# A hybrid decoder step on one core: lists ranked side by side, six raw buffers late in the value pass, and one convolution piece moved

## The reference

```python
xn = rmsnorm(x);  q, k, v, val, gate = split(xn @ w_in)
A  = sliding_window_attention(q, k, v)          # window 128, 8 heads, 2 key heads, learned sinks
glu = val * sigmoid(gate)                       # 512 channels
C  = silu(layer_norm(causal_depthwise_conv31(glu))) @ pw
h  = x + concat(rmsnorm(A), rmsnorm(C)) @ w_out
y  = h + PEER(rmsnorm(h))
```

```python
s = einsum(q, keys)                              # token, head, half, 128 keys
ts, ti = top_k(s, 16)                            # 16 lists of 128 for each token
best, pos = top_k(ts[half 0] + ts[half 1], 16)
act = gelu(u[idx] @ x) * softmax(best);  y = act @ v[idx]
```

## Time and profile before

| | |
|---|---|
| median of 3 runs | 1666.12 us (1665.33 to 1666.69) |
| profiled execution | 1666.06 us |
| its span | 1664.2 us |
| PE busy | 1622.5 us, 97% of the span |
| DVE busy | 1406.8 us, 85% |
| ACT busy | 825.9 us, 50% |
| DMA over the span | 480.42 MB, 289 GB/s mean |

### The profile page before, as it was taken

The page is one execution under the profiler, slowest core; times in us unless marked ns, Lnnn a source line. Parts: engine busy times, 40 slices in busy tenths (PEclk is TensorE's granted clock), DMA queues, the critical chain, the costliest instruction groups (busy, mean ns, idle before and its releaser), DMA issues.

```text
span 1664.2 us, 23162 instructions
## 1 busy us (share of the span) xinstructions
PE 1622.5 (97%) x8269; PEld 1387.7 (83%) x8269; DVE 1406.8 (85%) x2709; ACT 825.9 (50%) x1361; POOL 564.5 (34%) x414
## 2 busy tenths in 40 slices
PE   8998999999999999999999999999999999999998
PEld 6875555687999999999999999997777777777787
DVE  2178877877878999989999999969988989889896
ACT  5532333342244444449999999963333333333332
POOL 0000000010003344435454554534545545545450
PEclk9999999999999999999999999999999999999999
DMA  7113322253437899988999999999999999999994
GB/s 221 56 51 39 30 76 89 65 170 121 150 112 292 327 318 343 359 286 329 396 392 399 395 402 394 404 400 401 397 395 403 404 403 397 403 403 392 404 374 155
DMA packets 154504, 480.42 MB, mean 289 GB/s; under 512 B 25951, under 2 KB 42783, under 8 KB 152215
## 3 DMA queue, kind: packets, MB, share of 16 engines
q1 hardware_dynamic: 96791, 252.43, 42.9%
q0 software_dynamic: 55296, 201.35, 31.6%
q10 hardware_dynamic: 2304, 25.17, 3.6%
HBM read 424.99 MB, written 53.64 MB: 288 GB/s over the span
## 4 chain that ended last, share of the span: by engine, by line
PE 73%; DVE 13%; DMA 9%; ACT 2%; issue 2%; POOL 0%; DVEq 0%; SPq 0%; ACTq 0%; POOLq 0%
PE ps L858 26%; PE ps L1002 20%; DMA raw<-in_v 8%; PE ps L978 5%; PE ps L812 5%; PE ps L617 5%; PE ps L601 5%; DVE lo L1617 3%; PE ps L688 2%; DVE acc L1783 1%; DVE ring L1779 1%; ACT hi L1126 1%; DVE cacc L1463 1%; PE ps L629 1%; PE ps L640 1%
## 5 line engine op out<-in xcount | busy, mean ns | idle before, releaser
L1126 ACT ACTIVATE hi<-raw 128x1024 fp32r<-128x1024 f32 x236 | 249.6, 1058 | 367.5 <-PE ps L1002 232.1
L1387 POOL DMA_INDIRECT ring<-in_u,idx x192 | 271.8, 1415 | 421.8 <-DVE hu L1779 263.3
L1387 POOL DMA_INDIRECT ring<-in_v,idx x192 | 280.1, 1459 | 266.9 <-DVE acc L1783 253.7
L1617 DVE TENSOR_TENSOR lo<-raw,hi 128x1024 fp32r<-128x1024 f32 x236 | 288.6, 1223 | 87.3 <-ACT hi L1126 74.1
L858 PE MATMUL ps<-xh,lo 128*128 128x384 f32 x1024 | 342.7, 335 | 0.0
L858 PE MATMUL ps<-xh,hi 128*128 128x384 f32 x864 | 295.1, 342 | 4.2 <-DVE lo L1617 4.2
L858 PE MATMUL ps<-xl,hi 128*128 128x384 f32 x864 | 288.8, 334 | 0.0
L1002 PE MATMUL ps<-hi,ah 128*128 128x512 f32 x768 | 242.8, 397 | 7.5 <-DVE al L1927 7.2
L1783 DVE SCALAR_TENSOR_TENSOR acc<-ring,hu,acc 128x1024 f32<-128x1024 f32 x192 | 245.3, 1277 | 0.1
L1002 PE MATMUL ps<-lo,ah 128*128 128x512 f32 x768 | 241.2, 395 | 0.0
L1002 PE MATMUL ps<-hi,al 128*128 128x512 f32 x768 | 241.2, 395 | 0.0
(11 more groups left out here) (237 smaller groups left out, 2161.9 us busy)
## 6 DMA issues: line engine op xcount, KB each, us to landing
raw<-in_uT SPq DMA_DIRECT2D x128, 512.0 KB, 7.1
raw<-in_v SPq DMA_DIRECT2D x128, 512.0 KB, 8.5
wring<-in_wblk SPq DMA_DIRECT2D x58, 512.0 KB, 3.5
gate_matrix<-Gs ACTq DMA_DIRECT2D x16, 1536.0 KB, 10.5
gelu_matrix<-gest SPq DMA_DIRECT2D x62, 384.0 KB, 8.9
gel<-gelu_matrix SPq DMA_DIRECT2D x62, 384.0 KB, 8.7
Gl_odd<-gate_matrix SPq DMA_DIRECT2D x32, 384.0 KB, 10.4
Gl_even<-gate_matrix SPq DMA_DIRECT2D x24, 384.0 KB, 11.1
```

The source lines that it names most:

```text
L1126: nc.scalar.activation(high_of(s), raw[:, s % RAWS, :], ACT.Copy).then_inc(s_hi, 1)
L1387: pool.indirect_dma_start(ring[:, r % SLOTS, :], None, table, bass.IndirectOffsetOnAxis(idx[:, t, c:c + 1], 0)).then_inc(g_in[r % SLOTS], 16)
L1617: nc.vector.tensor_tensor(lo[:, s % 2, :], raw[:, s % RAWS, :], high_of(s).bitcast(F32), ALU.subtract).then_inc(s_lo, 1)
```

## The change

The change has three parts.

1. `conv_a(7)` moves from before `glu_out(3)` and `unit_max(4)` to behind them.
2. `rank` takes several lists and issues each of the five steps for all of them, with one wait per step. `ranks_b` passes its three lists together. `ranks_a` takes two score blocks at a time, waits for both, ranks two lists of the last prompt tile and one of the samples, and raises `s_l1` by two.
3. From v tile 19 on there are six raw buffers. The three more lie in `Gl_a`. When tile 18 is done SP loads tiles 21 to 24, and from then on tile n + 6 when tile n is done. `raw_use` gives slot and use count for each tile.

```diff
+RAWS_V = 6
+DEEP = NKEY + JG + RAWS
+def raw_use(s):
+    if s < DEEP:
+        return s % RAWS, s // RAWS + 1
+    slot = (s - DEEP) % RAWS_V
+    return slot, (s - DEEP) // RAWS_V + 1 + (DEEP // RAWS if slot < RAWS else 0)
...
-CONV_AT = [0, 1, 2, 3, 4, 6, 8]
+CONV_AT = [0, 1, 2, 3, 4, 6, 7]
...
+        more_raw = Gl_a.rearrange("p b j t -> p (b j t)")
+        def raw_of(s):
+            slot, _ = raw_use(s)
+            return raw[:, slot, :] if slot < RAWS else more_raw[:, (slot - RAWS) * D:(slot - RAWS + 1) * D]
...
-                if n + RAWS < NKEY:
+                deep = NKEY + n >= DEEP
+                if n + (RAWS_V if deep else RAWS) < NKEY:
                     sp.wait_ge(s_lo, NKEY + n + 1)
-                    load_raw(NKEY + n + RAWS)
+                    load_raw(NKEY + n + (RAWS_V if deep else RAWS))
+                if NKEY + n == DEEP - 1:
+                    for extra in range(RAWS, RAWS_V):
+                        load_raw(DEEP + extra)
...
             glu_out(3)
             unit_max(4)
+            conv_a(7)
             conv_a(8)
...
-            def rank(s, v, x):
-                link(nc.vector.max(v[:, 0:8], s))
-                link(nc.vector.max_index(x[:, 0:8], v[:, 0:8], s))
...
+            def rank(lists):
+                steps = (lambda s, v, x: nc.vector.max(v[:, 0:8], s),
...
+                for step in steps:
+                    for one in lists:
+                        ins = step(*one)
+                    link(ins)
...
-                m = A_ORDER[k]
...
+                for i in (k, k + 1):
+                    bank, n = use[f"sca{A_ORDER[i]}"]
+                    dve.wait_ge(F[bank], n)
+                h = k // 2
+                rank([(sm[:, i % 2, 0, :], tsv[:, TA, A_ORDER[i], :], tsi[:, TA, A_ORDER[i], :]) for i in (k, k + 1)]
+                     + [(sm[:, h % 2, 1, :], tsv[:, TB, h, :], tsi[:, TB, h, :])])
+                dve.sem_inc(s_l1, 2)
```

More of the change, by code:

```diff
@@ L415, in hymba_peer @@
         s_gst = [sem(f"gate_block_stored{i}") for i in range(2)]
-        r_in = [sem(f"raw_landed{i}") for i in range(RAWS)]
+        r_in = [sem(f"raw_landed{i}") for i in range(RAWS_V)]
+        more_raw = Gl_a.rearrange("p b j t -> p (b j t)")
+        def raw_of(s):
+            slot, _ = raw_use(s)
+            return raw[:, slot, :] if slot < RAWS else more_raw[:, (slot - RAWS) * D:(slot - RAWS + 1) * D]
         s_hi = sem("hi_ready")
@@ L480, in load_raw @@
                     src = v_d[v * P:(v + 1) * P, :]
-                sp.dma_start(raw[:, s % RAWS, :], src).then_inc(r_in[s % RAWS], 16)
+                sp.dma_start(raw_of(s), src).then_inc(r_in[raw_use(s)[0]], 16)
             def store_gelu(k):
@@ L1123, in high @@
             def high(s):
-                act.wait_ge(r_in[s % RAWS], 16 * (s // RAWS + 1))
-                nc.scalar.activation(high_of(s), raw[:, s % RAWS, :], ACT.Copy).then_inc(s_hi, 1)
+                slot, landed = raw_use(s)
+                act.wait_ge(r_in[slot], 16 * landed)
+                nc.scalar.activation(high_of(s), raw_of(s), ACT.Copy).then_inc(s_hi, 1)
             act.wait_ge(s_at, 6)
@@ L1616, in low @@
                     dve.wait_ge(s_hud, s - 1)
-                nc.vector.tensor_tensor(lo[:, s % 2, :], raw[:, s % RAWS, :], high_of(s).bitcast(F32),
+                nc.vector.tensor_tensor(lo[:, s % 2, :], raw_of(s), high_of(s).bitcast(F32),
                                         ALU.subtract).then_inc(s_lo, 1)
@@ L1646, in _ @@
                 second_norm(c, 0, DT, rs[:, 0, 0:DT])
-            def rank(s, v, x):
-                link(nc.vector.max(v[:, 0:8], s))
-                link(nc.vector.max_index(x[:, 0:8], v[:, 0:8], s))
-                link(nc.vector.match_replace(s, v[:, 0:8], s, LOW))
-                link(nc.vector.max(v[:, 8:16], s))
-                link(nc.vector.max_index(x[:, 8:16], v[:, 8:16], s))
+            def rank(lists):
+                steps = (lambda s, v, x: nc.vector.max(v[:, 0:8], s),
+                         lambda s, v, x: nc.vector.max_index(x[:, 0:8], v[:, 0:8], s),
+                         lambda s, v, x: nc.vector.match_replace(s, v[:, 0:8], s, LOW),
+                         lambda s, v, x: nc.vector.max(v[:, 8:16], s),
+                         lambda s, v, x: nc.vector.max_index(x[:, 8:16], v[:, 8:16], s))
+                for step in steps:
+                    for one in lists:
+                        ins = step(*one)
+                    link(ins)
             def ranks_b(*ms):
@@ L1659, in ranks_b @@
                     dve.wait_ge(F[bank], n)
-                    for t in range(DTI):
-                        rank(sm[:, m % 2, t, :], tsv[:, t, m, :], tsi[:, t, m, :])
+                    rank([(sm[:, m % 2, t, :], tsv[:, t, m, :], tsi[:, t, m, :]) for t in range(DTI)])
                     dve.sem_inc(s_l1, 1)
             def ranks_a(k):
-                m = A_ORDER[k]
[L1667 to L1672, removed]
+                for i in (k, k + 1):
[5 more added lines that the diff above has]
+                dve.sem_inc(s_l1, 2)
             def picks(t, lows, rows=()):
@@ L1850, in _ @@
             ranks_b(*range(11, NM))
-            for k in range(NM):
+            for k in range(0, NM, 2):
                 ranks_a(k)
```

## The result

The changed kernel takes 1657.38 us, the median of 5 runs (1656.19 to 1659.16), against 1666.69 (5 runs) for the kernel before. The ratio is 0.9944, 95% interval 0.9932 to 0.9956: 9.3 us faster. The forecast was 1655.0. The profiled execution took 1656.79 us, its span is 1655.0.

The account below looks back on a forecast made before the run. The prediction took PE's idle or lower-clock time on the chain as what could be won, with DMA also full in the value pass. 2.7 + 3.4 + 5 = 11.1 us off 1666.06 gave 1655.0 us, range 1650.5 to 1661.

Parts of the forecast that it names:

- edit 3: Value pass: six raw buffers from tile 19 on win 5 us of PE's 6.9 us of waits; bounds -3 to +6.9.
- Edit 1: Attention and convolution: conv_a(7) behind the gated product ends DVE's two waits, 4.1 us less 1.4 of clock: 2.7 us.
- The loss of 1.4 us: Two means behind PE's new 2 to 3 us gap run at a lower clock, charged at 1.4 us.
- Edit 2: Ranking: lists side by side remove PE's 1.37 us wait and the low clock behind it, 3.4 us; bounds -7 to +4.
- The 1.42 us of clock: Products behind PE's 1.37 us wait at 338.71 took 6.62 us against 5.20 at full clock; 1.42 us to win.
- The second part's handoff: Second ranking part: releasing two score blocks together makes a 5.4 us cycle, covered by PE's 6.76; costed at nothing.
- Rival 2: Ranking: side by side gains nothing, the handoff stalls PE some 7 us at its first U tiles; 1665.4 us, chance 0.06.
- rival 1: Value pass: bandwidth decides, raw tiles late as often, six raw buffers give 1 us; 1659 us, chance 0.20.
- the unused leads of gathers, activations and gates: Value pass, a source of the six buffers' gain: 3 to 5 us of transfers put off to the end.
- the line running dry: Value pass, a source of the six buffers' gain: places where SP's stream runs dry, an estimated 3 us.
- Rival 3: Value pass: six raw tiles in line delay gate loads, deciding from about 21 us landing, 5 us x 6 groups; 1683, chance 0.06.
- Rival 4: Whole kernel: more than forecast, all 6.9 us of value-pass waits go and no clock is lost; 14.6 us, 1651.5, chance 0.10.

Follow-up runs that it names:

- e_out4: The changed kernel with unit_out(4) moved ahead of conv_a(11) on DVE; ratio 0.9944 (0.9931 to 0.9958) to the kernel before.
- c_base: The changed kernel with unit_out(4) ahead of conv_a(11) and unit_out(5) ahead of conv_b(3) on DVE; median 1654.94 us, ratio 0.9929 to the kernel before.

## Why the prediction was right, and where it was not

The total was 2.4 us too low and inside the range. That it came so near is partly luck: edit 3 gave 3.4 us less than forecast, and 1.2 us in the u pass that these runs tie to no edit made up a part of that. Step by step:

**Edit 1, 2.7 us: the size right (2.70 in the pair, 2.8 over the four kernels each), the place wrong.** Forecast: both of DVE's waits go, the last copy comes 4.1 us earlier, a new gap of PE before the first mean, a lower clock behind it. The first two came true, the copy with 4.10 us. But "now PE will be through its taps at about 191" failed: PE was held at 182.91 by a PSUM bank, lost 2.12 us and some 1.7 us of clock (1.86 and 1.92 us for products that take 1.06 and about 1.1 at full clock), and came to the mean at 195.05 instead of 193.6. The loss of 1.4 us that I charged was therefore the right sum for a different reason. The step that failed is that I moved PE's whole queue forward with its taps, and asked of each of its instructions only whether its data were there, not whether its bank was free. The "about 191" has no working of its own: the last tap ended at 197.63 before, and 4.5 us less are 193.1. The rest would be clock, which the forecast charged for the new gap and did not credit for the old one: behind the 5.81 us gap the first 32 products of the taps took 10.74 us (151.96 to 162.70), in the changed kernel 8.87. `e_out4` brought the forecast's own gap to light, with 1.7 us for the clock in the place of 1.42.

**Edit 2, 3.4 us: 3.84 in the profiled pair, of which 2.3 are sure.** The wait and the slack in the short operations behind it are worth 2.2 to 2.4 us in every kernel. The 1.42 us of clock came as 1.46 in this pair, but the kernel before pays it only in some executions. Three lists in 4.1 us were forecast as 4.2, and it gives nothing by itself, since PE paces that stretch. The second part's handoff is there and covered as costed: the first u tile starts straight behind the last scores, and PE has no wait up to 480 us, past its third u tile. Rival 2 is out. The Trainium skill (VectorE: DVE Perf Modes, The DRAIN you can't avoid) says that leaving out semaphores between instructions does not save the pipe's flush, and adds that an instruction that is not held starts earlier. Here three independent MAX8 of 0.28 us take 0.68 together, so they start 0.20 apart: the trace agrees with the addition and not with the rule.

**Edit 3, 5 us: 1.6.** This is the term that was mis-sized, and rival 1 had about its size (1 us), though raw tiles were late less often and not as often: PE waited six times instead of ten. The failed step reads: "the unused leads of gathers, activations and gates, 3 to 5 us of transfers put off to the end". Gathers did not give up their lead: they land in 8.7 us instead of 8.1, while the loads of SP's queue take twice as long (gates 18.8 instead of 11.4). The longer line only stood in front of itself. The other source, the line running dry, did close: in fortieths of 1190 to 1594 us the rate fell to 367 GB/s before and never falls below 400 after. But 404 instead of 400 GB/s there is 1.7 MB, about three tiles, and most of it is only moved earlier. Over the whole v pass both kernels move 209 MB, at 380 and 381 GB/s on the mean; the last 28 us before ran at 105 GB/s and the last 26 after at 57, which is 1.4 MB less. Where the 1.6 us come from in detail stays open. The Trainium skill (DMA: Bandwidth & Descriptors, Queues, rings and completion order) has the DMA engines take packets from their queues in turn; by that rule a queue gets no larger share by having more in line, and the landings agree. I had the rule and the share of 1.03 in hand and gave them 0.20. PE's idle time beyond tile 19 was 4.5 us, between the 2.5 that were to show the forecast right and the 5 that were to show it wrong. Rival 3 showed at one place of six: the multiply of a group's first tile waited 0.90 us for its gates, at 1301.59, where rival 3 had 5 us for each group. Gate loads landed in up to 23.1 us, more than the 21 from which I let it decide. Rival 4 needed 6.9 us here.

**Not forecast, 1.2 us in the u pass.** The stage took 643.9 us here and 644.7 to 647.7 in the other kernels that leave it alone, so this is no effect of the change that these runs can show.

## What to carry to other kernels

Where PE waits although buffers, DVE and ACT have slack, halve the bytes once. If the waits vanish with the old number of buffers, look for bytes to move before you add buffers: eight gathers shifted to a stage with more room shortened this pass by 9 to 10 us and cost 3.7 there, where three more buffers gave 1.6. When an edit lets an engine run ahead, go through its queue and ask of each instruction what frees its PSUM bank. A wait that was level before becomes the next stall, and it can be read in the old trace: the transposes at 187.01 stood 0.15 us behind the copy there too. A gap of PE of one or two microseconds may cost about as much again in clock, so a gap that an edit only moves may give nothing back, as in `e_out4`.

## What the runs showed of the hardware

- One wait, two clocks. PE's wait of 1.4 us at 337 to 340 us left the clock at 1.00 in two executions and brought it down in two (0.58 over 341 to 344 us), 1.5 us of difference. The same at the first batches of gates: a wait of 2.03 us, and then twelve products in 1.58 us in the changed kernel, 2.87 in `c_base`. Why one execution keeps the clock and another does not is open.
- An idle time under "issue" can be a wait for a PSUM bank that DVE gives back with a semaphore increment of its own: 2.12 us, gone in `e_out4`. The profile names no releaser for it.
- Issuing a DMA is not free when much is in line: SP took 0.33 us for a raw load with three buffers; with six it took 1.92 us at the median (3.80 at most) for those into `raw` and 0.63 (3.66 at most) for those into `Gl_a`.
- PE's idle time understates what late data cost: 7.2 us shown over the v pass, 12.1 lost against the same products without any wait. The waits of PE's weight loads for DVE's low part come nearer, 11.7 us over the same pass (8.5 after, where 10.6 were lost).
- Over 1184 to 1587 us, inside the v pass, the core moves 404 GB/s at a share of 1.03 with six buffers in every kernel with full gathers, and 400 or 401 with three. Over the whole pass, where its end is counted in, it is 381 and 380.
